# One more wait at the end of GpSimd's program, in front of its closing drain

## The chip, the cores and the metric

One core of a Trainium2 chip (trn2) runs the whole kernel. The metric is the device time of one execution in microseconds; lower is better. Three executions of the kernel before took 1090.13, 1089.12 and 1090.13 us.

## What is computed

The reference is one inference step of a hybrid decoder layer: a normalisation and projections, a pooling mixer beside stick-breaking attention, an output projection, and then a hierarchical mixture of experts. The part at issue is the last one, where every token goes through two of 32 experts and the weighted results are added to the token's row:

```python
def channel_mixer(x, norm_g, w_group, w_expert, w_gate, w_up, w_down):
    B, T, D = x.shape
    n = rms_norm(x, norm_g).reshape(B * T, D)
    return x + hier_moe(n, w_group, w_expert, w_gate, w_up, w_down).reshape(B, T, D)

...
    def expert_block(args):
        xb, e = args
        return (jax.nn.silu(xb @ w_gate[e]) * (xb @ w_up[e])) @ w_down[e]

    ys = lax.map(expert_block, (xs, blk_exp)).reshape(P, D)
    out = jax.ops.segment_sum(ys * row_w[:, None], row_tok, num_segments=T + 1)[:T]
```

## The kernel before, in words

The program is written engine by engine, in the order in which each engine runs it; semaphores order the engines against each other. The first half computes projections, pooling, attention and the output projection. The second half works through the experts as blocks `b` = 0 to 31 of 96 token rows each (`NE` = 32, `CAP` = 96). For a block, GpSimd gathers the 96 normalised rows from DRAM into `xg` (`gather`, line 1244, an indirect DMA), TensorE transposes them and multiplies by the expert's gate and up weights, ScalarE and VectorE make the hidden rows, TensorE multiplies by the down weights, ScalarE and VectorE write the weighted result into `yo`, and GpSimd adds the rows of `yo` to `y_all` in DRAM by an indirect DMA that adds (`scatter`, line 1254). SyncE (SP) issues the loads of the expert weights.

The results already stand in `y_all` as residuals when the first block's rows are added. Two adding scatters could reach the same row, so GpSimd waits in `moved(b)` for the landing of scatter `b` before it goes on. Every adding scatter raises the semaphore `s_sc` ("block_scattered") by 16 when all of it has landed. The last block is scattered in two halves of the columns (`scatter_half`, line 1295), so there are 33 adding scatters in all: 31 whole blocks and two halves. `scatters(NE - 1)` is the count of `s_sc` after the last of them, 16 * 33 = 528.

Behind the two halves GpSimd's program has a branch at line 1302 on the number of overflow blocks, `n_over`. With these inputs there are none, and the branch skips lines 1303 to 1312. What follows for every engine is the end of the `nc.Block()` of line 851: a closing drain on each engine and a barrier, in which the engines report on one semaphore, GpSimd collects the reports and then releases them all.

SP's program ends with its own waits, the last of which is line 1122:

```python
            sp.wait_ge(s_vst, 16 * 2 * NT)
            sp.wait_ge(s_sc, scatters(NE - 1))
```

Of the kernel before, what the change touches and what calls it, by code (L numbers as in the profile page):

```python
# [53 lines left out]
NE, NGRP, EPG = 32, 4, 8  # L54
# [39 lines left out]
def hybrid_step(nc, x_prompt, x_sample, cache_k, cache_v, state_pool, page_table, meta_tokens,  # L94
# [359 lines left out]
    for i in range(NU + 2):  # L454
# [11 lines left out]
        if 1 <= i <= NU:  # L466
            ring += [(("sum", i - 1, j), "act") for j in range(len(groups(i - 1)))]
    ring_at = {what: n for n, (what, _) in enumerate(ring)}

    def freed_by(n):  # L470

        eng = ring[n][1]
        return eng, len([1 for _, e in ring[:n + 1] if e == eng])
# [24 lines left out]
    def sem(name):  # L498
        return nc.alloc_semaphore(name)
# [111 lines left out]
    s_sc = sem("block_scattered")  # L611
# [21 lines left out]
    NV = 2 * NT  # L633
    NQK = 4 * NT
    assert all(kind == "v" for kind, _, _ in steps[:NV])

    def v_steps(t):
# [101 lines left out]
    def scatters(b):  # L739

        return 16 * (b + 1) if type(b) is int and b < NE - 1 else 16 * (b + 2)
# [109 lines left out]
    with nc.allow_non_contiguous_dma(reason="small vectors and broadcasts"), blk as block:  # L851
# [273 lines left out]
        def _(pool):  # L1125
# [112 lines left out]
            def gather(b):  # L1238

                i = b % 2  # L1240
                pool.wait_ge(s_ix, 1 if b < NE else b - NE + 2)
                if b >= 2:
                    pool.wait_ge(s_xt if b < 4 else s_xc, b - 1)
                pool.indirect_dma_start(out=xg[i][0:CAP, :], out_offset=None, in_=n_scr,  # L1244
                                        in_offset=bass.IndirectOffsetOnAxis(ap=rows_named(b, gidx), axis=0),
                                        bounds_check=T - 1, oob_is_err=False).then_inc(s_gl[i], 16)

            def scatter(b):

                pool.wait_ge(s_ya, copies(b))  # L1250
                pool.wait_ge(s_yd, copies(b))
                if b >= NE:
                    pool.wait_ge(s_sx2, b - NE + 1)
                pool.indirect_dma_start(out=y_all,  # L1254
                                        out_offset=bass.IndirectOffsetOnAxis(ap=rows_named(b, sidx), axis=0),
                                        in_=yo[b % 2][:, :], in_offset=None, compute_op=ALU.add,
                                        bounds_check=T - 1, oob_is_err=False).then_inc(s_sc, 16)

            def moved(b):

                if b < NE - 3 or b >= NE:
                    pool.wait_ge(s_gl[(b + 3) % 2], 16 * ((b + 3) // 2 + 1))
                pool.wait_ge(s_sc, scatters(b))
# [38 lines left out]
            with pool.If(n_over > 0):  # L1302
                for b in range(3):
                    gather(NE + b)
                for i in range(2):
                    pool.wait_ge(s_gl[(NE + i) % 2], 16 * ((NE + i) // 2 + 1))
                pool.wait_ge(s_sc, scatters(NE - 1))
                for o in range(OVB):
                    with pool.If(n_over > o):
                        gather(NE + o + 3)  # L1310
                        scatter(NE + o)
                        moved(NE + o)

        @block.scalar
        def _(act):
# [1635 lines left out]
```

## Time and profile before

| what | us |
|---|---|
| executions shown | 1090.13, 1089.12, 1090.13 |
| profiled execution, its own time | 1090.1 |
| its span, from the first instruction to the last | 1090.1 |
| TensorE matmuls, busy | 1045.2 |
| VectorE, busy | 544.4 |
| ScalarE, busy | 309.3 |
| GpSimd, busy | 174.6 |

The profile's times are microseconds from the start of the span. An engine's name with a q behind it (POOLq, SPq) is the engine's sequencer: its waits, branches and drains, which don't count as busy. POOL is GpSimd, SP is SyncE, ACT is ScalarE, DVE is VectorE, PE is TensorE and PEld its weight loads. The span ends with the last instruction of the closing barrier, so whatever the barrier waits for is part of the time.

### The profile page before, as it was taken

How to read it: one execution, taken by the hardware profiler on the slowest of the kernel's cores; microseconds unless marked ns; L12 is line 12 of the kernel's file. 1: busy time of each engine (PE TensorE's matmuls, PEld its weight loads, DVE VectorE, ACT ScalarE, POOL GpSimd, SP SyncE). 2: the span in 40 equal slices, each digit the busy share in tenths (PEclk: the TensorE clock that was granted, in tenths of full speed). 3: DMA queues.
4: the chain of work that ended last, by engine and by line, in shares of the span. 5: the costliest groups of instructions: out<-in, count | busy, mean ns of one | idle time of the engine just before them, and what ended most of it. 6: DMA issues, size and time to landing. Idle time of an engine off the chain costs nothing.

```text
span 1090.1 us, 29226 instructions
## 1 busy us (share of the span) xinstructions
PE 1045.2 (96%) x12774; PEld 826.0 (76%) x12774; DVE 544.4 (50%) x1052; ACT 309.3 (28%) x592; POOL 174.6 (16%) x160
## 2 busy tenths in 40 slices
PE   8999999999999999999999999999999988898996
PEld 7999999966666549899876898756898556565665
DVE  5327654378875543444734544555455534343431
ACT  6323332266775552222411011101110111101011
POOL 1001200599200000100010111111111111111102
PEclk9999999999999999999989999999999999999999
DMA  7356785000116467767899999999999999999994
GB/s 244 109 166 211 217 272 155 1 13 2 40 31 211 146 232 251 245 220 277 312 351 393 379 383 385 386 383 375 386 379 382 379 390 388 392 390 389 390 389 111
DMA packets 85816, 293.19 MB, mean 269 GB/s; under 512 B 13425, under 2 KB 44849, under 8 KB 60069
## 3 DMA queue, kind: packets, MB, share of 16 engines
q1 hardware_dynamic: 78277, 273.30, 67.2%
q0 software_dynamic: 7280, 17.58, 6.8%
q8 instruction: 103, 1.69, 0.6%
q10 hardware_dynamic: 128, 0.39, 0.1%
q14 instruction: 28, 0.23, 0.1%
HBM read 272.98 MB, written 42.87 MB: 290 GB/s over the span
## 4 chain that ended last, share of the span: by engine, by line
PE 73%; DMA 18%; DVE 4%; SPq 2%; ACT 1%; issue 1%; POOL 0%; ACTq 0%; POOLq 0%
PE bank L2827 20%; DMA w_all<-in_w_up 18%; PE bank L2375 12%; PE bank L2612 8%; PE bank L2418 4%; PE bank L2844 4%; PE bank L2584 3%; PE bank L2547 3%; PE bank L2848 3%; PE bank L2456 3%; SPq L1042 2%; PE bank L2852 2%; DVE keep L1887 1%; PE bank L2693 1%; PE bank L2479 1%
## 5 line engine op out<-in xcount | busy, mean ns | idle before, releaser
L2827 PE MATMUL bank<-w_all,xeT 128*32 128x256 f32 x6144 | 345.6, 382 | 22.2 <-DMA w_all<-in_w_up 19.2
L2827 PEld LDWEIGHTS bank<-w_all,xeT 128*32 128x32 f32 x6144 | 254.4, 111 | 107.0 <-issue 27.9
L2202 DVE STREAM_TRANSPOSE xeT<-xg 32x256 f32<-32x256 f32 x360 | 156.5, 435 | 97.0 <-DMA xg<-n_scr,tab 91.8
L2844 PE MATMUL bank<-w_all,hT 128*32 128x256 f32 x744 | 165.6, 379 | 0.0
L2848 PE MATMUL bank<-w_all,hT 128*32 128x512 f32 x744 | 129.3, 592 | 0.0
L1887 DVE TENSOR_TENSOR_SCAN keep<-keep,unseen 128x1024 f32<-128x1024 f32 (+7 forms) x64 | 94.8, 1514 | 37.8 <-ACT keep L1439 37.7
L2375 PE MATMUL bank<-w_hi,xh 128*128 128x256 f32 x376 | 108.1, 287 | 0.0
L2375 PE MATMUL bank<-w_hi,xl 128*128 128x256 f32 x376 | 105.5, 281 | 0.0
L2375 PE MATMUL bank<-w_lo,xh 128*128 128x256 f32 x376 | 105.5, 280 | 0.0
L2844 PEld LDWEIGHTS bank<-w_all,hT 128*32 128x32 f32 x744 | 81.8, 110 | 30.3
L1681 ACT ACTIVATE sgl<-bank 128x384 f32<-128x384 f32 x32 | 15.7, 490 | 304.2 <-PE bank L2827 304.2
L2612 PE MATMUL bank<-wo_hi,cat 128*128 128x256 f32 (+1 forms) x384 | 89.0, 321 | 0.4 <-issue 0.4
L1254 POOL DMA_INDIRECT out_y_all<-yo,tab x31 | 44.4, 1432 | 204.9 <-ACT yo L1692 199.8
L2852 PE MATMUL bank<-w_all,hT 128*32 128x256 f32 x744 | 76.4, 379 | 0.0
L1244 POOL DMA_INDIRECT xg<-n_scr,tab x32 | 31.5, 986 | 264.4 <-issue 243.3
L2375 PEld LDWEIGHTS bank<-w_hi,xh 128*128 128x128 f32 x376 | 70.8, 188 | 0.6 <-issue 0.2
L2375 PEld LDWEIGHTS bank<-w_hi,xl 128*128 128x128 f32 x376 | 71.1, 189 | 0.0
L2375 PEld LDWEIGHTS bank<-w_lo,xh 128*128 128x128 f32 x376 | 70.8, 188 | 0.0
L2612 PEld LDWEIGHTS bank<-wo_hi,cat 128*128 128x128 f32 x384 | 64.2, 189 | 5.6 <-issue 0.7
L2234 DVE TENSOR_SCALAR yo<-bank,gtab 96x256 f32<-96x256 f32 x31 | 14.9, 480 | 105.3 <-PE bank L2844 105.3
L2215 DVE TENSOR_TENSOR hid<-sgl,bank 128x384 f32<-128x384 f32 x32 | 27.3, 852 | 77.2 <-PE bank L2827 63.3
L1690 ACT ACTIVATE yo<-bank,gtab 96x512 f32<-96x512 f32 x31 | 21.1, 682 | 144.8 <-PE bank L2844 144.8
(307 smaller groups left out, 1505.9 us busy)
## 6 DMA issues: line engine op xcount, KB each, us to landing
w_all<-in_w_down SPq DMA_DIRECT2D x64, 1024.0 KB, 30.2
w_all<-in_w_gate SPq DMA_DIRECT2D x64, 1024.0 KB, 32.6
w_all<-in_w_up SPq DMA_DIRECT2D x64, 1024.0 KB, 8.9
k_scr<-in_cache_k SPq DMA_DIRECT2D x32, 256.0 KB, 3.3
v_scr<-in_cache_v SPq DMA_DIRECT2D x32, 256.0 KB, 3.5
pgk<-k_scr SPq DMA_DIRECT2D x32, 256.0 KB, 3.9
w_raw<-in_w_in SPq DMA_DIRECT2D x7, 1024.0 KB, 7.1
pgv<-v_scr SPq DMA_DIRECT2D x4, 1024.0 KB, 6.6
```

What stands on the lines that cost most here:

```text
L1254: pool.indirect_dma_start(out=y_all, out_offset=bass.IndirectOffsetOnAxis(ap=rows_named(b, sidx), axis=0), in_=yo[b % 2][:, :], in_offset= ...
L1887: dve.tensor_tensor_scan(back, back, unseen[:, NK - w:NK][:, ::-1], 1.0, ALU.mult, ALU.max).then_inc(s_p, 1)
L2202: last = dve.transpose(xeT[i][rows_of(s), :, rows_of(g)], lane[:, :, s, :])
L2375: last = pe.matmul(proj_ps(s)[0:r, :], a[:, k, row0(t):row0(t) + r], b[n % 2][:, k, :], start=(k == 0 and j == 0), stop=(k == KT - 1 and j ...
L2418: last = pe.matmul(wide_ps(s)[:, 0:cols], a[n % 2][:, k, c:c + P], b[:, k, lo:lo + cols], start=(k == 0 and j == 0), stop=(k == KT - 1 and ...
L2456: last = pe.matmul(z_ps(a)[:, lo:lo + n], qT[rows, hp, row0(t):row0(t) + P], kT[rows, hp, lo:lo + n], start=True, stop=True)
L2547: last = pe.transpose(t_ps(n)[0:keys, k, :], keep_of(u, a)[:, P * i:P * i + keys], ident[:, :])
L2612: last = pe.matmul(out_ps(s)[0:r, :], cat_tile(a, t)[:, k, 0:r], b[n][:, k, :], start=(k == 0 and j == 0), stop=(k == KT - 1 and j == 2))
L2827: lasts = [pe.matmul(pair_ps(i)[rows_of(q), g, :, :], xeT[i][:, k, rows_of(g)], pair_of(b, i, k, q), start=(k == 0 and g != 1), stop=(k == ...
L2844: return pe.matmul(y_right_ps(g), hT[:, ft, rows_of(g)], w[ft // 2][:, ft % 2, DA:D], start=first and g != 1, stop=ends, skip_group_check= ...
L2848: pe.matmul(y_left_ps[rows_of(g), :], hT[:, ft, rows_of(g)], w[ft // 2][:, ft % 2, 0:512], start=first, stop=ends, skip_group_check=True)
L2852: lasts = [pe.matmul(y_mid_ps[rows_of(g), :], hT[:, ft, rows_of(g)], w[ft // 2][:, ft % 2, 512:DA], start=first, stop=ends, skip_group_che ...
```

## The change

GpSimd's program gets one line at its end, behind the branch on the overflow blocks and in front of the closing drain: it waits until `s_sc` has the count of all adding scatters of the blocks 0 to 31, the same count for which SP waits in line 1122.

```diff
@@ -1310,6 +1310,7 @@
                         gather(NE + o + 3)
                         scatter(NE + o)
                         moved(NE + o)
+            pool.wait_ge(s_sc, scatters(NE - 1))
 
         @block.scalar
         def _(act):
```

## Rows read from the trace of the kernel before

**Rows 1.** The page: span, busy time of the engines, the chain that ended last
```profile
span 1090.1 us, 29226 instructions
...
PE 73%; DMA 18%; DVE 4%; SPq 2%; ACT 1%; issue 1%; POOL 0%; ACTq 0%; POOLq 0%
```

**Rows 2.** The chain, last 9 us: start, us, what
```profile
1081.72 0.58 ACT yo L1700
...
1082.87 0.05 POOLq L1302
1082.92 0.17 issue
1083.09 1.40 POOL out_y_all L1295
```

**Rows 3.** Line 851, the closing drains and barrier: duration ns min/median/max, first and last start
```profile
L851 POOLq EVENT_SEMAPHORE  x2: 17/17/17, 1089.9 to 1090.0; - x2
L851 ACTq DRAIN  x1: 8/8/8, 1082.7 to 1082.7; - x1
L851 DVEq DRAIN  x1: 61/61/61, 1083.2 to 1083.2; - x1
L851 POOLq DRAIN  x1: 6542/6542/6542, 1083.3 to 1083.3; - x1
L851 PEldq DRAIN  x1: 73/73/73, 1086.4 to 1086.4; - x1
L851 SPq COMPARE_BRANCH  x1: 41/41/41, 1086.8 to 1086.8; - x1
L851 SPq DRAIN  x1: 7/7/7, 1087.0 to 1087.0; - x1
L851 SPq EVENT_SEMAPHORE  x1: 17/17/17, 1090.1 to 1090.1; - x1
```

**Rows 4.** Line 1122, SP's wait for the last scatter, same columns
```profile
L1122 SPq EVENT_SEMAPHORE  x1: 28/28/28, 1086.7 to 1086.7; - x1
```

**Rows 5.** Windows of the tail: stretch, length, busy by engine, granted clock, DMA share, GB/s
```profile
1084.49:1086.74 2.25, 0.00 (x0) 0.00 (x0) 0.00 (x0) 0.00 (x0) 0.00 (x1) 0.55 0.54 64
1086.74:1090.11 3.37, 0.00 (x0) 0.00 (x0) 0.00 (x0) 0.00 (x0) 0.00 (x0) 0.50 0.02 5
```

**Rows 6.** Line 2935, the drains of the program's start, columns as in rows 3
```profile
L2935 DVEq DRAIN  x1: 10/10/10, 0.1 to 0.1; - x1
...
L2935 POOLq DRAIN  x1: 187/187/187, 0.4 to 0.4; - x1
L2935 POOL MEMSET const-uint8-127<- x1: 115/115/115, 0.4 to 0.4; 128x1 uint8 x1
```

**Rows 7.** GpSimd's indirect DMAs by line: busy us, mean ns, idle before
```profile
L1254 POOL DMA_INDIRECT out_y_all<-yo,tab x31 | 44.4, 1432 | 204.9 <-ACT yo L1692 199.8 <-issue 5.1
L1244 POOL DMA_INDIRECT xg<-n_scr,tab x32 | 31.5, 986 | 264.4 <-issue 243.3 <-PE bank L2800 12.1 <-DMA out_y_all<-yo,tab 8.9
...
L1295 POOL DMA_INDIRECT out_y_all<-yo,lidx x2 | 2.8, 1404 | 1.3 <-issue 1.3
```

**Rows 8.** Lines 842 and 1302, the branches on the overflow count, columns as in rows 3
```profile
L842 PEldq COMPARE_BRANCH  x1: 5184/5184/5184, 1081.2 to 1081.2; - x1
L842 ACTq COMPARE_BRANCH  x1: 50/50/50, 1082.5 to 1082.5; - x1
...
L1302 POOLq COMPARE_BRANCH  x1: 53/53/53, 1082.9 to 1082.9; - x1
```

**Rows 9.** Line 1295's two half scatters, issue to landing
```profile
DMA to landing us min/median/max: 3.6/4.3/5.0
```

## The prediction

> **What bounds the kernel now.** The page comes first [rows 1]: a span of 1090.1 us, whose chain is mostly TensorE and weight loads. None of that is touched; the edit stands behind the last scatter, so only the last few microseconds are in question. For these I read the end of the chain [rows 2], then the sequencers' rows of the closing drains [rows 3], which the chain view doesn't contain.
>
> The chain ends with the second half scatter's instruction on GpSimd, which starts at 1083.09 and takes 1.40, so it is over at 1084.49 [rows 2]. The span goes on to 1090.1. What fills these 5.6 us is in [rows 3]: ScalarE, VectorE, TensorE and SP have their closing drains at 1082.7, 1083.2, 1086.4 and 1087.0, each of 7 to 73 ns. GpSimd's drain starts at 1083.3 and takes 6.54 us, to about 1089.9, where GpSimd's first semaphore instruction of the barrier follows at once; SP's release is at 1090.1. So **GpSimd's closing drain is what ends the kernel**, with 0.2 us of barrier behind it, and every other engine waits for it.
>
> How does that drain stand to the data? SP waits in line 1122 for the very count that the change names, and passes at 1086.7 [rows 4]. Data have landed there. The DMA engines are busy before that moment (share 0.54) and idle after it (0.02) [rows 5]. So of the drain's 6.54 us, 1.15 lie beside the scatter's own instruction (to 1084.49), 2.25 beside the landing (to 1086.74), and 3.15 come after everything that the trace shows.
>
> **The change part by part.** It adds one wait on GpSimd. Nothing is queued behind it but the drain and the barrier, no DMA is moved past it, and no other engine waits for GpSimd at this point except in the barrier. It takes nothing away: the drain stays.
>
> The wait passes when SP's does, at 1086.7. SP's sequence behind it is wait, branch, drain: 1086.7, 1086.8, 1087.0 [rows 3, 4]. I take the same for GpSimd, so its drain starts at 1087.0; by its own last branch, from 1082.9 to the drain at 1083.3 [rows 3, 8], it would be 1087.2. Before, it started at 1083.3. **The start moves by 3.7 us.** The whole question is how long a drain lasts that starts after the landing.
>
> The trace has no such drain. Bounds from the nearest rows:
>
> - *Below:* GpSimd's drain at the program's start took 187 ns, beside a memset that itself began at 0.4 [rows 6]. No indirect DMA had been issued by then. SP's closing drain took 7 ns [rows 3], but SP is another engine.
> - *Above:* the drain as it stands, 6.54 us [rows 3].
> - *Between:* its 5.39 us from the end of the scatter's instruction (1089.88, which is 1083.34 + 6.54, less 1084.49), if the part before was only a wait for that instruction; and its 3.15 us after the landing.
>
> The break-even is 1089.9 - 1087.0 = 2.9 us: a drain longer than that makes the kernel slower. I take **5.4 us**. The reason: had the drain only waited for the data, it would have ended soon after 1086.7, as SP's wait on the same landing did, in 28 ns. It went on for 3.15 us with no transfer left to wait for, so it does work of its own, or steps through something. What separates it from the drain of 187 ns at the start is what GpSimd issued in between: 31 + 32 + 2 = 65 indirect DMAs [rows 7]. If the drain steps through all of them, one by one, whether long landed or not, 5.39 us / 65 = 83 ns for each, an estimate; the three last are landed before their turn comes, so their landing costs nothing now and waiting for it first saves nothing. Such a drain costs the same wherever it starts, as long as GpSimd is otherwise idle. This is nearest to the row itself, which is why I choose it over the two lower values.
>
> Sum, against the profiled execution's 1090.1: drain from 1087.0 to 1092.4, barrier 0.2, end 1092.6; with the later start 1092.8. I say **1092.7**, 2.6 us or 0.24% more. The median of the runs shown, 1090.13, stands 0.02 from that execution, so no correction. If the drain takes the full 6.54 from its start, the end is 1087.0 + 6.54 + 0.2 = 1093.7, or 1093.9 with the later start.
>
> A rule that speaks against this: the row has 6.54 us for GpSimd's closing drain against 7 to 73 ns for the other four [rows 3]. The Trainium skill (VectorE: DVE Perf Modes, section The DRAIN you can't avoid) says that the drains at a program's two ends are a constant of about 12 ns on all five engines. By that rule the drain after the landing would be nothing and the kernel would end near 1087.2; four rows agree roughly, GpSimd's row disagrees by a factor of 500.
>
> **The rivals.**
>
> *A tail behind the landing, unchanged.* The drain waits for the data and then needs a fixed 3.15 us. If that runs from the landing, nothing moves: 1090.1. If it runs from the drain's start at 1087.0 to 1087.2, the end is 1087.0 + 3.15 + 0.2 = 1090.35, or 1090.55. For it: the landing lies inside the drain, as it must if the drain waits for it. Against it: nothing in the trace stands between landing and end that would need that time, and the start's drain did without it. No measurable change either way.
>
> *The drain is long only because it begins with transfers in flight* (faster). Its mechanism would be a check that comes round rarely: found busy once at 1083.3 to 1084.5, it looks again late. Place: the 3.15 us behind the landing. Started with everything landed, it would cost the 0.19 us of the start: 1087.0 + 0.19 + 0.2 = 1087.4, to 1087.6 with the later start, 2.5 to 2.7 us or 0.24% less. It decides if the drain takes under 0.7 us (then over 0.2% is gained); between 0.7 and 2.9 the gain is there but too small. For it: 3.15 us of silence fits a sleeping check as well as work, and the one idle drain that the trace has is short. Against it: that drain had no DMAs behind it, so it doesn't test this. The skill's 12 ns, above, would come out on this side too.
>
> *The new end of the program isn't in instruction memory* (slower). GpSimd would reach the drain by one more jump. TensorE's jump over its overflow code took 5.18 us, ScalarE's 50 ns, GpSimd's 53 ns [rows 8]. Paid on top of the wait, it would put the end at 1097.9 with a 5.4 us drain. SP's jump at the same place took 41 ns, so I give this little.
>
> That the wait does nothing is excluded: its count isn't reached before 1086.7 on SP [rows 4], and the half scatters took up to 5.0 us from issue to landing [rows 9].
>
> **How the numbers follow.** Drain costs the same wherever it starts: 0.60. Tail behind the landing, no change: 0.22. Short drain, faster: 0.15. Instruction load: 0.03. The runs of this kernel spread by 1.0 us, and about 0.2%, 2.2 us, is what a measurement can tell from no change. The forecast's 2.5 to 3.8 us lie barely above that line, so of its 0.60 I count 0.45 as slower and 0.15 as within. The second case is within (0.22). Of the third, 0.13 is faster and 0.02 within; the fourth is slower. Sum: faster 0.13, within 0.39, slower 0.48.
>
> The range holds the forecast and the no-change case: its high end is 1093.9 and a little spread, 1094.1; its low end is 1090.1 less 0.7 of the spread between the shown runs, 1089.4. Left out are the short drain and the instruction load, 0.18. The forecast's own range is 1092.4 to 1094.1.
>
> **What would show it.** In the changed kernel's rows: GpSimd's wait passing at about 1086.7; its drain starting near 1087.0 and lasting 5.4 us (forecast), 6.5 (no part was waiting), 3.15 (tail) or under 0.7 (short). Its end must be 0.2 us before the span's. A short drain makes the prediction wrong in sign; a late start of the drain with a long branch ahead of it would be the instruction load. If the drain's length follows the number of indirect DMAs issued, the estimate of 83 ns each holds; if it doesn't, the mechanism is wrong even where the time is right.

## The result, and the profile after

The changed kernel takes 1092.66 us (median of 22 executions, 1090.73 to 1094.25), the kernel before 1090.13 us in the same number (1088.33 to 1093.15). The ratio is 1.0021, with a 95% interval of 1.0015 to 1.0027: **slower by 0.21%**, 2.3 us (1.6 to 2.9), just over the 0.2% that the prediction set as the line. The medians lie 2.5 us apart.

The rows that answer to [rows 3] and [rows 4] are those of line 851 and line 1122 in the changed kernel: engine, operation, count, duration in ns (min/median/max), first and last start in us.

```profile
L851 POOLq EVENT_SEMAPHORE  x2: 17/17/17, 1090.4 to 1090.5; - x2
...
L851 POOLq COMPARE_BRANCH  x1: 38/38/38, 1084.8 to 1084.8; - x1
L851 SPq COMPARE_BRANCH  x1: 41/41/41, 1084.9 to 1084.9; - x1
L851 POOLq DRAIN  x1: 5383/5383/5383, 1085.0 to 1085.0; - x1
L851 SPq DRAIN  x1: 7/7/7, 1085.0 to 1085.0; - x1
L851 SPq EVENT_SEMAPHORE  x1: 17/17/17, 1090.5 to 1090.5; - x1
```

```profile
L1122 SPq EVENT_SEMAPHORE  x1: 28/28/28, 1084.8 to 1084.8; - x1
```

GpSimd's wait has no row of its own. A branch of line 851 that the kernel before doesn't have starts at 1084.8, when SP's wait passes too, so the wait seems to be held there. The drain starts at 1085.0 and takes 5.383 us, and the barrier's 0.1 to 0.2 us follow. Before, the drain took 6.542 us, of which 1.15 lay beside the last scatter's instruction; the remaining 5.39 are the same 5.38 as now. **The drain's own work has not become shorter or longer; it only starts later.**

How much later is to be read against the last scatter's instruction. In the changed kernel's chain its end is at 1081.06 + 1.40 = 1082.46:

```profile
1080.84 0.05 POOLq L1302
1080.89 0.17 issue
1081.06 1.40 POOL out_y_all L1295
```

Before, the work of the drain could begin at 1084.49, with that instruction's end [rows 2]. Now it begins at 1085.0, 2.5 us behind 1082.46: 2.34 us until the landing and 0.2 for the branch. That is the loss: from the end of that instruction to the end of the span it is 5.62 us before (1090.11 - 1084.49) and 8.11 now (1090.57 - 1082.46). The clock positions of the two traces can't be compared directly: in the changed kernel's profiled execution everything ahead of the last scatter happened to be 2.0 us earlier, inside the 4.8 us by which executions of the kernel before differ.

The windows of the changed kernel's tail show what the wait was for, and what came behind it (stretch, length, busy time of PE, PEld, DVE, ACT, POOL, granted clock, DMA share, GB/s):

```profile
1082.46:1084.80 2.34, 0.00 (x0) 0.00 (x0) 0.00 (x0) 0.00 (x0) 0.00 (x1) 0.50 0.52 65
1084.80:1090.57 5.77, 0.00 (x0) 0.00 (x0) 0.00 (x0) 0.00 (x0) 0.00 (x0) 0.50 0.00 0
```

For 5.77 us no engine computes and the DMA engines' share is 0.00; 5.38 of them are GpSimd's drain, the rest the branch and the barrier.

### The profile page after: what moved, and what is told of

Its sections match the earlier page's. It is cut to its first block, busy times and chain, and to the rows that moved or that the text cites. A ratio compares the mean times of both kernels' runs of the same rounds, so it can differ in the third digit from the quotient of the medians.

```text
span 1090.6 us, 29227 instructions
## 1 busy us (share of the span) xinstructions
PE 1043.0 (96%) x12774; PEld 826.5 (76%) x12774; DVE 543.6 (50%) x1052; ACT 309.7 (28%) x592; POOL 174.6 (16%) x160
## 4 chain that ended last, share of the span: by engine, by line
PE 73%; DMA 18%; DVE 4%; SPq 2%; ACT 1%; issue 1%; POOL 0%; ACTq 0%; POOLq 0%
PE bank L2828 20%; DMA w_all<-in_w_up 18%; PE bank L2376 12%; PE bank L2613 8%; PE bank L2419 4%; PE bank L2845 4%; PE bank L2585 3%; PE bank L2548 3%; PE bank L2849 3%; PE bank L2457 3%; SPq L1042 2%; PE bank L2853 2%; DVE keep L1888 1%; PE bank L2694 1%; PE bank L2480 1%
```

## The experiments

The theory was that the drain steps through every DMA that GpSimd has issued, landed or not. Its rivals were a price by rows or descriptors, and a fixed price once any such DMA was issued. Four variants of the changed kernel change the number of DMAs or of rows.

**Half the rows, as many DMAs.** The expectation on record:

> The changed kernel, with the gathers of blocks 0 to 31 cut from 96 rows to 48; the other half of each gathered tile keeps old rows, so that part of the result is left out. Still 65 indirect DMAs, but 4704 rows in place of 6240 (65 x 96). Count theory (the closing drain steps through every DMA that GpSimd issued, 5.383 us / 65 = 83 ns each, landed or not): drain 5.4 us, as in the changed kernel. Row theory (the price goes by rows or descriptors, 5.383 us x 4704 / 6240): 4.06 us. Fixed theory (one price after any indirect DMA): 5.4 us. Waiting theory (the drain's length hangs on how lately data landed): no figure, but it starts after the landing here too, so 5.4 us.

```diff
-                pool.indirect_dma_start(out=xg[i][0:CAP, :], out_offset=None, in_=n_scr,
-                                        in_offset=bass.IndirectOffsetOnAxis(ap=rows_named(b, gidx), axis=0),
+                rows = CAP // 2 if b < NE else CAP
+                pool.indirect_dma_start(out=xg[i][0:rows, :], out_offset=None, in_=n_scr,
+                                        in_offset=bass.IndirectOffsetOnAxis(ap=rows_named(b, gidx)[0:rows, :], axis=0),
```

Line 851 of this kernel:

```profile
L851 POOLq DRAIN  x1: 5383/5383/5383, 1074.4 to 1074.4; - x1
```

The same 5.383 us to the nanosecond, with a quarter of the rows gone. The row theory's 4.06 us is out. (The single execution took 1081.80 us, the one of the next variant 1060.77; both move less data all along the second half, so these times say nothing about the drain.)

**Fewer DMAs.**

> The changed kernel, with the gathers of blocks 4 to 31 left out; those blocks work on the rows of blocks 2 and 3, so most of the mixture's result is left out. 37 indirect DMAs are left (4 gathers, 33 adding scatters). Count theory: drain 37 x 83 ns = 3.06 us. Row theory: 3552 rows, also 3.06 us. Fixed theory: 5.4 us.

```diff
             def gather(b):
...
+                if 4 <= b < NE:
+                    return
```

(the waits on the landings of these gathers ask for the last one that is left; GpSimd's waits in front of the gathers stay). Line 851:

```profile
L851 POOLq DRAIN  x1: 3097/3097/3097, 1055.7 to 1055.7; - x1
```

37 DMAs, 3.10 us for the forecast 3.06. A fixed price is out.

**More DMAs, indirect and plain.**

> The changed kernel with one further indirect gather of 16 short rows of 64 bytes into a spare tile behind each of the scatters 0 to 29: 95 indirect DMAs, 6720 rows. Count theory: drain 95 x 83 ns = 7.87 us. Row theory: 5.383 x 6720 / 6240 = 5.80 us. Fixed theory: 5.4 us.

> As the one with 30 further gathers, but the 30 further DMAs are plain ones issued by GpSimd, 16 rows of 64 bytes each. Count theory, if any DMA of GpSimd counts: drain 95 x 83 ns = 7.87 us; if only the indirect ones count: 5.4 us. Row theory: 5.80 us. Fixed theory: 5.4 us.

```diff
                 scatter(b)
                 if b < NE - 2:
+                    pool.wait_ge(s_sx2, 16 * b)
+                    pool.indirect_dma_start(out=extra[0:16, :], out_offset=None,
+                                            in_=n_scr.rearrange("t (c d) -> (t c) d", d=16),
+                                            in_offset=bass.IndirectOffsetOnAxis(ap=rows_named(b, gidx)[0:16, :], axis=0),
+                                            bounds_check=T - 1, oob_is_err=False).then_inc(s_sx2, 16)
                     moved(b)
```

(`extra` is a spare tile and `s_sx2` a semaphore that only overflow blocks would use; in the other kernel the DMA is `pool.dma_start(extra[0:16, :], n_scr[0:16, 0:16])`). The closing section stands in line 852 here. With further gathers, then with plain DMAs:

```profile
L852 POOLq DRAIN  x1: 7833/7833/7833, 1085.0 to 1085.0; - x1
```

```profile
L852 POOLq DRAIN  x1: 7833/7833/7833, 1085.5 to 1085.5; - x1
```

7.83 us for the forecast 7.87, and the kind of DMA makes no difference. Nor is it GpSimd's waits that are counted: here each further DMA brings one wait along, while in the kernel with fewer DMAs the waits stayed, and the price of one DMA is the same. From 37 to 65 to 95 DMAs the drain grows by 2.286 and 2.450 us, 81.6 and 81.7 ns for each further one; what is left over is 5383 - 65 x 81.7 = 73 ns. One execution of each took 1094.83 and 1095.43 us beside one of 1089.80 of the kernel before.

**Does a drain clear the list?** If so, a drain in time in which GpSimd idles would leave little for the closing one. The edits below are made to the kernel before, without the new wait, except where it is named.

> The kernel before (without the new wait), with one further drain on GpSimd behind the landing of scatter 29, where GpSimd then idles for some 7 us until the next block is ready. From the three counts measured so far a drain takes 75 ns and 81.7 ns for each DMA. Clearing theory (a drain takes landed DMAs off the list, so the next one steps only through those issued since): the early drain 75 + 62 x 81.7 = 5.14 us, hidden; the closing one has 3 DMAs and ends 0.1 to 0.3 us behind the last landing; 1087.2 us for 1090.1, ratio 0.997. History theory (every drain steps through all DMAs ever issued): the closing drain ends 5.4 us behind the last scatter's instruction as before, ratio 1.000.

```diff
                 if b < NE - 2:
                     moved(b)
+                if b == NE - 3:
+                    pool.drain()
```

The early drain is line 1289, the closing one line 851:

```profile
L1289 POOLq DRAIN  x1: 5124/5124/5124, 1069.8 to 1069.8; - x1
```

```profile
L851 POOLq EVENT_SEMAPHORE  x2: 17/17/17, 1085.7 to 1085.7; - x2
...
L851 POOLq DRAIN  x1: 3525/3525/3525, 1082.0 to 1082.0; - x1
...
L851 SPq DRAIN  x1: 7/7/7, 1085.6 to 1085.6; - x1
```

```profile
L1122 SPq EVENT_SEMAPHORE  x1: 27/27/27, 1085.4 to 1085.4; - x1
```

62 DMAs take 5.124 us in the early drain. It delays nothing: GpSimd's engine still idles 14.6 us until ScalarE has the next block's rows ready, as it did for 14.4 in the kernel before:

```profile
1077.64 1.40 POOL L1254 DMA_INDIRECT out_y_all<-yo,tab  x1 [14.61 <-ACT yo L1694]
```

The closing drain starts at 1082.0, with the last half still in flight, and ends at 1085.5, 0.1 to 0.2 us behind the landing at 1085.4 instead of 3.15; it is now really a wait for the data, and SP's drain at 1085.6 starts as late as GpSimd's ends. The kernel takes 1087.13 us (8 executions) beside 1090.32 (24), ratio 0.9973 (0.9962 to 0.9983): **this version beats both kernels**, by 2.9 us (1.9 to 4.1) against the one before. The trace has the same gain. The last scatter's instruction ends here at 1081.78 + 1.40 = 1083.18, and the span at 1085.9, 2.7 us later, where the kernel before needs 5.62:

```profile
1081.78 1.40 POOL L1297 DMA_INDIRECT out_y_all<-yo,lidx  x1 [0.55 <-issue]
```

**The early drain with the new wait.**

> As the kernel with one early drain, and with the new wait in front of the closing drain. Clearing theory: the closing drain starts 0.2 us behind the landing and takes 75 + 3 x 81.7 = 320 ns; 1087.5 us for 1090.1, ratio 0.9976, some 0.3 us more than without the wait. History theory: closing drain 5.383 us, 1092.6 us, ratio 1.0023.

```profile
L851 POOLq COMPARE_BRANCH  x1: 38/38/38, 1083.6 to 1083.6; - x1
...
L851 POOLq DRAIN  x1: 303/303/303, 1083.8 to 1083.8; - x1
```

Three DMAs, 303 ns for the forecast 320. Here the tail is the one that a reader of the change might expect: a wait, a short drain, the end. 1087.51 us (11 executions), ratio 0.9983 (0.9974 to 0.9992). Against the version without the wait it should cost 0.3 us; the medians differ by 0.4 and the intervals overlap, so the timing alone doesn't show it. The traces agree with it: from the end of the last scatter's instruction (1080.03 + 1.40) to the end of the span at 1084.3 it is 2.9 us, 0.2 more than without the wait.

```profile
1080.03 1.40 POOL L1297 DMA_INDIRECT out_y_all<-yo,lidx  x1 [0.55 <-issue]
```

**A drain behind every block, and four drains.**

> The kernel before with a drain on GpSimd behind the landing of every scatter from 0 to 29. Clearing theory: the first drain has 5 DMAs, 483 ns; the others 2 (one gather, one scatter), 238 ns; the last one before the end 1, 157 ns; each delays the next gather by that, which has several us to spare; the end as with one early drain, ratio 0.997. History theory: the drains grow by 163 ns from block to block up to 5.14 us; they delay the gathers of the late blocks by some 4 us, the end stays as it was, ratio 1.000 or more.

> The kernel before with drains on GpSimd behind the landings of scatters 3, 11, 19 and 29. DMAs issued by then: 11, 27, 43 and 62; since the drain before: 11, 16, 16 and 19. Clearing theory: 0.97, 1.38, 1.38 and 1.63 us. History theory: 0.97, 2.28, 3.59 and 5.14 us.

The edits put `if b < NE - 2: pool.drain()` and `if b in (3, 11, 19, 29): pool.drain()` in the same place. Line 1289 in the first and in the second:

```profile
L1289 POOLq DRAIN  x30: 119/201/469, 588.8 to 1068.0; - x30
```

```profile
L1289 POOLq DRAIN  x4: 959/1346/1589, 636.1 to 1068.0; - x4
```

Five DMAs 469 ns, two 201, one 119; 11 DMAs 959 ns, 16 1344 and 1349 (the row gives the middle of the two), 19 1589. Nothing grows with the history: a drain is charged only for the DMAs issued since the one before, as if it took what has landed off a list. These drains are 14 to 38 ns shorter than 75 + 81.7 n for n DMAs, so their fixed part is 37 to 61 ns, less than the 72 to 74 that the three long closing drains left. The kernel with 30 drains takes 1087.71 us (11 executions), ratio 0.9979 (0.9969 to 0.9989), which isn't to be told from one early drain; the one execution with four took 1085.36.

The kernel with 30 drains shows one more thing, in its rows of lines 1304 (the branch on the overflow count) and 851:

```profile
L1304 POOLq COMPARE_BRANCH  x1: 58/58/58, 1080.1 to 1080.1; - x1
```

```profile
L851 POOLq DRAIN  x1: 692/692/692, 1083.3 to 1083.3; - x1
```

3.2 us lie between the branch and the closing drain, where the kernel before has 0.4 [rows 3, 8]. GpSimd's program is 30 instructions longer there. That looks like the prediction's rival of the end of the program that isn't in instruction memory, but the cause wasn't tried out and stays open. It cost nothing, since the landing came at 1083.8.

## Why the prediction was right

*What bounds the tail.* It held: GpSimd's drain ends the kernel, before and after, with the barrier behind it.

*The start of the drain.* The earlier of the two values held: 0.2 us behind the wait, as on SP. The other, from the branch of line 1302, was too long.

*The drain's length.* This was the term on which all hung, and 5.4 us was taken for what measured 5.383. The reading behind it held as well: the part of the old drain beside the scatter's instruction was a wait for that instruction, the rest a price that depends on neither the landing nor the rows. The 6.54 us of the other end of the range would have needed the drain to step through its list while the instruction still ran.

*The price of one DMA.* 83 ns was the drain divided by 65, with no fixed part. The slope over three counts is 81.7 ns, with 37 to 74 ns fixed. The mechanism named for it was a step for every indirect DMA that GpSimd issued. That the drain's length goes by the number of DMAs, though all have landed when it starts, is shown from 1 to 95 of them. Two things the experiments add to it: plain DMAs count as much as indirect ones, and only those since GpSimd's last drain count. What the sequencer does for each DMA isn't shown, nor that it goes through them one by one.

*The rivals.* A fixed tail behind the landing would have been 3.15 us in the changed kernel; it was 5.38. The short drain needed under 0.7 us. Its idea that a drain after the landing can be short is right only where few DMAs have been issued since the last drain (303 ns with three), and there the kernel was no slower without the wait. The end of the program outside instruction memory needed a long branch ahead of the drain; GpSimd's new branch took 38 ns. The rule of the Trainium skill (VectorE: DVE Perf Modes, section The DRAIN you can't avoid), a constant of about 12 ns on all engines, fits SP's and ScalarE's closing drains here (7 and 8 ns). The page says it of the runtime's own drains at a program's two ends, and the prediction took it for the block's closing drains. GpSimd's drains, closing or early, ranged from 119 ns to 7.83 us, mostly by the number of its DMAs.

*The baseline.* One step of the working was wrong and did no harm. The prediction took the span of the profiled execution, 1090.1, for its time, as the table of times before does, and found it 0.02 us from the median. In every later execution whose span is on record the time is 1.7 to 1.9 us above the span (1092.38 beside 1090.6, 1081.80 beside 1080.0), so that execution's time was probably near 1091.9, on the slow side of the kernel's spread. That the span came out equal to the median time was chance. The sum was a difference, +2.6 us, and so it stands: 1090.13 + 2.5 gives 1092.6 on the scale of the times.

*The chances.* 0.48 for slower by over 0.2% was about fair for an effect of 0.21%: the interval reaches down to 0.15%.

## What to carry to other kernels

Before a wait is added in front of something that seems to wait already, ask what that thing does besides waiting: here the drain's own steps ran beside the landing, and the wait put them behind it. In these traces a GpSimd drain costs about 82 ns for each DMA that GpSimd has issued since its last drain, and the program's end pays for it: 5.38 us for 65. A drain placed where GpSimd idles anyway took the price off the end here, 2.9 us of it. When the end of a span is idle on all engines, read the sequencers' rows, which the chain of waits leaves out.

## What was not expected of the hardware

The drain's length repeats to the nanosecond: 5383 ns in the changed kernel and in the one with half the rows, 7833 ns with 30 indirect DMAs more and with 30 plain ones. And DMAs issued more than 500 us earlier (the first at 545 of 1090 us in the kernel before), for whose landing GpSimd itself had long waited on semaphores, are still paid for at the end.
